# The laying out of substitution rows in the heads' delta rule: one fp32 matmul, or two fp32r matmuls over a high and a low part

## What is computed

```python
low = jnp.einsum('nbhik,nbhjk->nbhij', kb, kc) * decay_strict
t_inv = lax.linalg.triangular_solve(low + eye, eye, left_side=True, lower=True, unit_diagonal=True)
u = jnp.einsum('nbhij,nbhjv->nbhiv', t_inv, vb)
```

## Time and profile before

| | |
|---|---|
| median of 3 runs | 1622.85 us (1619.63 to 1623.05) |
| the profiled execution | 1618.03 us |
| its span | 1616.2 us |
| TensorE busy | 1586.6 us, 98% of the span |
| VectorE busy | 986.1 us, 61% |
| GpSimd busy | 154.3 us, 10% |

### The profile page before, as it was taken

How to read it: one execution, slowest core, us unless ns; L and a number is a source line. 1 busy time by engine, 2 the same in 40 slices (tenths; PEclk the granted TensorE clock), 3 DMA queues, 4 the chain that set the end, 5 groups by cost and what they waited for, 6 DMA issues and landing times.

```text
span 1616.2 us, 29865 instructions
## 1 busy us (share of the span) xinstructions
PE 1586.6 (98%) x11971; PEld 1435.0 (89%) x11971; DVE 986.1 (61%) x1685; ACT 636.7 (39%) x1094; POOL 154.3 (10%) x170
## 2 busy tenths in 40 slices
PE   7999999999999999999999999999999999799997
PEld 6887899999999999999999999999999998577765
DVE  5676447766867668577445654444498865533455
ACT  5666445442543425434332232222244434422422
POOL 0121000121112111121100001111100000000000
PEclk9999999999999999999999999999999999999999
DMA  7798754332433323333369975888813348978764
GB/s 274 251 296 261 239 136 121 80 95 56 118 94 79 94 65 107 95 77 106 81 166 235 246 186 140 218 218 210 218 48 107 93 127 299 363 257 289 243 247 163
DMA packets 344206, 274.64 MB, mean 170 GB/s; under 512 B 50953, under 2 KB 291490, under 8 KB 343090
## 3 DMA queue, kind: packets, MB, share of 16 engines
q1 hardware_dynamic: 321648, 256.48, 54.2%
q10 hardware_dynamic: 22466, 16.88, 3.8%
HBM read 229.50 MB, written 44.17 MB: 169 GB/s over the span
## 4 chain that ended last, share of the span: by engine, by line
PE 92%; DVE 3%; DMA 2%; issue 1%; ACT 1%; SPq 1%; ACTq 0%; DVEq 0%
PE pj L283 47%; PE pj L508 11%; PE dk L3009 6%; PE pj L2349 5%; PE dk L2349 3%; PE pj L2968 3%; PE pj L2976 1%; PE dk L2631 1%; DMA w_raw_co<-in_w_co_dram 1%; PE pj L2670 1%; PE dk L1955 1%; PE dk L1332 1%; PE dk L368 1%; PE pj L2653 1%; DVE q_both L2255 1%
## 5 line engine op out<-in xcount | busy, mean ns | idle before, releaser
L283 PE MATMUL pj<-a_hi,w_high 128*128 128x272 f32 x1664 | 364.6, 300 | 0.3 <-DVE w_low L267 0.2
L283 PE MATMUL pj<-a_hi,w_low 128*128 128x272 f32 x1664 | 343.6, 288 | 0.0
L283 PE MATMUL pj<-a_lo,w_high 128*128 128x272 f32 x1664 | 343.2, 288 | 0.0
L283 PEld LDWEIGHTS pj<-a_hi,w_high 128*128 128x128 f32 x1664 | 259.5, 189 | 12.7 <-issue 7.8
L283 PEld LDWEIGHTS pj<-a_lo,w_high 128*128 128x128 f32 x1664 | 261.4, 188 | 0.0
L283 PEld LDWEIGHTS pj<-a_hi,w_low 128*128 128x128 f32 x1664 | 260.1, 189 | 0.0
L267 DVE TENSOR_TENSOR w_low<-w_raw,w_high 128x2048 fp32r<-128x2048 f32 x68 | 155.4, 2286 | 77.0 <-ACT w_high L257 76.9
L257 ACT ACTIVATE w_high<-w_raw 128x2048 fp32r<-128x2048 f32 x68 | 130.4, 1917 | 73.6 <-PE pj L283 42.4
L283 PE MATMUL pj<-mix_hi,w_high 128*128 128x272 f32 x512 | 105.9, 288 | 0.1
L283 PE MATMUL pj<-mix_lo,w_high 128*128 128x272 f32 x512 | 105.4, 288 | 0.0
L283 PE MATMUL pj<-mix_hi,w_low 128*128 128x272 f32 x512 | 105.1, 287 | 0.0
(11 more groups left out here) (460 smaller groups left out, 2890.9 us busy)
## 6 DMA issues: line engine op xcount, KB each, us to landing
w_raw<-in_w_in_dram SPq DMA_DIRECT2D x48, 1024.0 KB, 5.8
w_raw_co<-in_w_co_dram SPq DMA_DIRECT2D x28, 1024.0 KB, 7.4
w_raw_wide<-in_w_ck_dram SPq DMA_DIRECT2D x16, 1024.0 KB, 6.9
w_raw_wide<-in_w_cv_dram SPq DMA_DIRECT2D x16, 1024.0 KB, 7.5
w_raw<-in_w_out_dram SPq DMA_DIRECT2D x16, 1024.0 KB, 6.9
keys_s<-keysT_scratch SPq DMA_DIRECT2D x7, 2048.0 KB, 10.2
values_s<-in_cache_mem_v_dram SPq DMA_DIRECT2D x28, 512.0 KB, 8.2
q_part<-in_w_cq_dram SPq DMA_DIRECT2D x48, 256.0 KB, 3.6
```

The lines of the kernel that those rows point to most:

```text
L283: mm = pe.matmul(pj[:, 2 * (q % 2) + b, 0:n], wt[:, k, :], x(k, o, n), start=(k == 0 and m == 0), stop=(k == KT - 1 and m == 2))
```

## The change

The strips are laid out by two fp32r matmuls per bank in place of one fp32 matmul. VectorE rounds `comp` to `comp_high`, subtracts it from `comp` for `comp_low`, and spreads `comp_high` over the strips `own_high`. GpSimd spreads `comp_low` over the strips `own_low`. TensorE waits for both and adds the two products in the same bank. The last strip gets four rows in place of three (60 elements in place of 45).

```diff
-strip_rows = lambda r: min(4, BLK - 1 - 4 * r)
+strip_rows = lambda r: 4
...
+        def own_strip(eng, dst, src, r):
+
+            m, w = strip_rows(r), strip_width(r)
+            return eng.tensor_tensor(dst, src[:, :, BLK - w:BLK].unsqueeze(2).to_broadcast([P, CH + 1, m, w]),
+                                     cst[:, C_E16 + 4 * r:C_E16 + 4 * r + m].unsqueeze(1).unsqueeze(3).to_broadcast(
+                                         [P, CH + 1, m, w]), ALU.mult)
...
                 dve.wait_ge(comp_ready, n + 1)
+                dve.tensor_copy(comp_high[:], comp[:]).then_inc(comp_cast, 1)
+                dve.wait_ge(comp_cast, n + 1)
+                dve.tensor_tensor(comp_low[:], comp[:], comp_high[:].bitcast(F32), ALU.subtract).then_inc(comp_split, 1)
                 for r in range(4):
-                    m, w = strip_rows(r), strip_width(r)
-                    a = dve.tensor_tensor(strip(own_row, r), comp[:, :, BLK - w:BLK].unsqueeze(2).to_broadcast([P, CH + 1, m, w]),
...
+                    a = own_strip(dve, strip(own_high, r), comp_high[:].bitcast(F32), r)
                 a.then_inc(own_ready, 1)
...
             if q == 1:
+                pool.wait_ge(comp_split, n + 1)
+                for r in range(4):
+                    a = own_strip(pool, strip_low(r), comp_low, r)
+                a.then_inc(own_rest, 1)
                 old()
...
-                blk = cst[:, C_BLK:C_BLK + P]
+                pe.wait_ge(own_rest, n + 1)
                 for b in range(2):
                     e = strip_size(b) + strip_size(b + 2)
-                    mm = pe.matmul(dk[:, b, 0:e], blk, own_row[:, b, 0:e], start=True, stop=True)
+                    pe.matmul(dk[:, b, 0:e], blk_r[:], own_high[:, b, 0:e], start=True, stop=False)
+                    mm = pe.matmul(dk[:, b, 0:e], blk_r[:], own_low[b][:, 0:e], start=False, stop=True)
```

More of the change, by code:

```diff
@@ L730, in build @@
         betab = take("betab", [TOK])
+        dd_at = take.pos[0]
         dd = take("dd", [2, TOK])
@@ L744, in build @@
         ksv = put("ksv", [2, P], F32, take.pos[0] - 2 * TOK + 4 * CH * T32)
-        own_row = put("own_row", [2, OWN_BANK], F32, take.pos[0] - 2 * TOK)
+        own_high = put("own_high", [2, OWN_BANK], F32R, take.pos[0] - 2 * TOK)
         assert 2 * OWN_BANK <= 2 * TOK
@@ L751, in build @@
         ones_r = take("ones_r", [P], F32R)
+        blk_r = take("blk_r", [P], F32R)
+        comp_high, comp_low = take("comp_high", [CH + 1, BLK], F32R), take("comp_low", [CH + 1, BLK])
+        own_low = [put("own_low0", [OWN_BANK], F32R, dd_at + TOK), put("own_low1", [strip_size(1) + strip_size(3)], F32R, vbk_at)]
+        assert OWN_BANK <= TOK and strip_size(1) + strip_size(3) <= SEQ
         SQ = put("sq", [2, TOK], F32, fold_at)
@@ L800, in build @@
         ks_taken, kqs_ready = sem("ks_taken"), sem("kqs_ready")
+        comp_cast, comp_split, own_rest = sem("comp_cast"), sem("comp_split"), sem("own_rest")
         kds_copied, vns_copied = Reused(squared, 7), Reused(rooted, 7)
@@ L1126, in strip, with strip_low @@
             return x[:, r % 2, o:o + n].rearrange("p (c j i) -> p c j i", c=CH + 1, j=strip_rows(r))
+        def strip_low(r):
+            o, n = (0 if r < 2 else strip_size(r - 2)), strip_size(r)
+            return own_low[r % 2][:, o:o + n].rearrange("p (c j i) -> p c j i", c=CH + 1, j=strip_rows(r))
+        def own_strip(eng, dst, src, r):
[3 more added lines that the diff above has]
+                                         [P, CH + 1, m, w]), ALU.mult)
         def substitute(eng, n):
@@ L1145, in dve_delta @@
                     dve.tensor_copy(ones_r[:], ones)
+                    dve.tensor_copy(blk_r[:], cst[:, C_BLK:C_BLK + P])
                 dve.wait_ge(qk_silu, n + 1)
@@ L1181, in dve_delta @@
                 dve.wait_ge(comp_ready, n + 1)
+                dve.tensor_copy(comp_high[:], comp[:]).then_inc(comp_cast, 1)
+                dve.wait_ge(comp_cast, n + 1)
+                dve.tensor_tensor(comp_low[:], comp[:], comp_high[:].bitcast(F32), ALU.subtract).then_inc(comp_split, 1)
                 for r in range(4):
-                    m, w = strip_rows(r), strip_width(r)
-                    a = dve.tensor_tensor(strip(own_row, r), comp[:, :, BLK - w:BLK].unsqueeze(2).to_broadcast([P, CH + 1, m, w]),
-                                          cst[:, C_E16 + 4 * r:C_E16 + 4 * r + m].unsqueeze(1).unsqueeze(3).to_broadcast(
-                                              [P, CH + 1, m, w]), ALU.mult)
+                    a = own_strip(dve, strip(own_high, r), comp_high[:].bitcast(F32), r)
                 a.then_inc(own_ready, 1)
```

## The result

The changed kernel took 1628.32 us (median of 8 runs) against 1622.74 us: ratio 1.0036, 95% interval 1.0019 to 1.0052. It is slower, as forecast, but by 5.6 us where 12.9 were expected.

A forecast was written before the change was run, and what follows sets the result against it. TensorE, busy 98%, was taken to bound the kernel, with VectorE's run to `t_next` only 0.06 us shorter in six heads; 10.2 us for heads 1 to 6, 1.44 and 1.23 made 12.9, so 1635.8 us, range 1625.5 to 1644.

The forecast's parts named there:

- TensorE saves 0.52 us per head, if it could be kept: TensorE's strip matmuls: four fp32r passes take 0.67 us in place of 1.19, 4.2 us in all.
- The cast and the subtraction delay the first strip by 0.40 us: VectorE ahead of its strips: two new instructions make the first strip start 0.40 us later, at 359.52.
- Whole instructions, in turns: VectorE's and GpSimd's strips, both reading two SBUF tensors, alternate by whole instructions; adds 1.24 us to VectorE's delay.
- Substitution starts 1.66 later: VectorE's first substitution step: the strips' whole delay of 1.66 us is carried over to it.
- Slack 0.06 us at `t_next`: TensorE's wait at `level32_p`, heads 1 to 6: VectorE's delay less 0.06 us makes TensorE late.
- 0.1 us per head for a broken stream: TensorE at a wait that binds: breaking its stream costs up to 0.2 us, taken as 0.1 per head.
- The sum: All heads: 1.70 us in each of heads 1 to 6, 1.44 in head 0, 1.23 in the last; together 12.9 us.
- No taking of turns: Rival, strips: VectorE's run through first, GpSimd's follow; VectorE late by 0.42 us, 3.0 us in all, 1625.8; chance 0.14.
- Dear short runs on GpSimd: Rival, GpSimd's strips: short runs cost 3 ns per column; 19.8 us in all, 1642.6; chance 0.17.
- Faster, because the wait does not decide: Rival, `level32_p`: TensorE passes the wait in time and keeps 0.52 us per head, 4.2 us, 1618.7; chance 0.06.
- The case that was forecast: Strips taking turns, GpSimd at 1.7 to 2.2 ns per column: 1635 to 1639 us; chance 0.63.
- the range for 8 in 10: Whole kernel time: from the case without turns, 1625.5, to a little above dear short runs, 1644 us.

The follow-up runs named there:

- high_only: Changed kernel with the low part left out (no cast, subtraction or low strips, one fp32r pass per bank); ratio 0.9986 against the kernel before.
- pool_later: Changed kernel with GpSimd's four strips made to wait for VectorE's last strip, nothing else; ratio 1.0105 against the kernel before.
- the second timing: The same changed kernel timed again without any edit against the kernel before; ratio 1.0056 (1.0035 to 1.0077).

## Why the prediction was right in kind and wrong in size

The direction, the mechanism and its place were right; the size was not, 12.9 us against 5.6 in the first comparison, 9.1 in the heads. The step that failed is the one from VectorE's delay to TensorE's: 1.66 us at the strips, carried over whole to the first step of the substitution and on to TensorE, at 1.70 us per head. The runs showed 1.49 us at `kds`, 1.27 at the first step and 1.18 at TensorE.

*TensorE saves 0.52 us per head, if it could be kept.* Right: 1.19 became 0.65, and high_only shows that it cannot be kept behind VectorE's list as it is.

*The cast and the subtraction delay the first strip by 0.40 us.* Right: it starts 0.40 us after the cast does (360.00 and 360.40), in the place where it started before.

*Whole instructions, in turns.* Right, by the forms' durations and by pool_later. The term was mis-sized: VectorE's strips got 1.08 us longer in place of 1.24 and 0.02. Read in the same way as above over all of head 1, GpSimd's first three strips cost 0.55 + 0.41 + 0.27 = 1.23 us (1.30 worked out) and VectorE's last three 0.24 + 0.17 + 0.08 = 0.49 (0.59): once it has its turn, VectorE needs hardly more than its columns at 1.04 ns, and I had added 0.05 us to each.

*"Substitution starts 1.66 later."* This is where it failed most. With the strips' true share `kds` is 1.49 us late, and the first step started only 1.27 us later. In the earlier trace rows the first step starts at 364.25, after the split's end at 364.10, because it waited there for TensorE's slow fp32 matmuls, which end at 364.11. The kernel before, VectorE and TensorE, head 1:

```profile
361.83 2.27 DVE L267 TENSOR_TENSOR w_low<-w_raw,w_high 128x2048 fp32r<-128x2048 f32 x1
```

```profile
362.76 1.35 PE L1348 MATMUL dk<-own_row,cst 128*128 128x440 f32 x4
```

In the changed kernel the last of the four matmuls is over by 365.28, and the first step starts at 366.40, just as the split runs out. high_only bears this out: there the first step starts 4.93 us after the first strip, against 5.13 before, with no added work on VectorE but the 15 elements of the last strip. I had called TensorE's step "in time" after the change and not asked whether it had been so before. So the shorter matmuls did pay something: 0.2 us per head, on VectorE's path.

*Slack 0.06 us at `t_next`, the delay paid nearly whole.* Right: in heads 5 and 6 `t_next` is 1.25 us later, and TensorE starts `level32_p` 31.22 to 31.23 us after the norms in place of 30.04, 1.18 us later. Over heads 1 to 6 it is 1.12 to 1.25.

*0.1 us per head for a broken stream.* Wrong: 1.25 less 0.06 is 1.19, so the break costs nothing there.

*The sum.* Per inner head 1.70 us became 1.18: 0.18 from the turns, 0.22 from the first step, 0.1 from the break, 0.02 from rounding. The seven heads and the last one together give 9.1 us. What remains down to 5.6 stands in no trace: the interval of the first timing ends at 8.4 us, the second timing gave 8.9. So 3.8 of the 7.3 us by which the forecast missed are accounted for, and the rest stays open.

*The rivals.* No taking of turns: excluded by the groups of L1142. Dear short runs on GpSimd: excluded; in pool_later 300 and 220 columns differ by 133 ns, 1.7 ns per column with runs of 15 and 11 elements. Faster, because the wait does not decide: excluded by high_only. The case that was forecast, 1635 to 1639 us, did not hold; the range for 8 in 10, 1625.5 to 1644, took in the measured 1628.3 only by its lower edge, which came from the excluded case without turns, and that is luck. The sum came out too high because the break and VectorE's fixed time, both unmeasured, were taken too large, and what the quicker matmuls give back to VectorE was put at nothing without a look at the rows before.

What stays open is the rule by which the turns are given. Among the strips it is first come, first served by the recorded starts (GpSimd's second at 361.37, VectorE's third at 361.58, in all eight heads and each of the three places); in pool_later the later record won in seven heads of eight. Whether GpSimd's order of strips (small ones first) would have changed anything wasn't tried.

## What to carry to other kernels

Ask of a saving on the busiest engine how far behind the next path is. Look for it at waits that cause no idle time yet: the distance between a producer's end and the wait it serves was 0.06 us here, and it decided more than the 0.5 us that was saved. An instruction moved to GpSimd is not taken off VectorE if both read two tensors from SBUF at that time; put it beside VectorE's work from PSUM, or on ScalarE. And when a step gets quicker, list who had been waiting for it before, since that is where its gain comes back.

## What the runs showed of the hardware

A GpSimd instruction of 140 columns took 2.82 us on average beside a VectorE instruction of 2.27 us, in seven heads of eight one that started 0.31 us later by the record. ScalarE's small activations with a scale column cost 0.23 us from start to start on average (16 in 3.68 us), from 0.25 us at 75 columns down to 0.20 us at 15.

In pool_later the 2.4 us for which TensorE stood idle in each head had a second price. In heads 2, 6 and 7 of eight the granted clock fell after it, to 1.2 GHz, and came back within 5 us; head 2, in windows of 2 us (busy time by engine, then the granted clock):

```profile
434.00:436.00 2.00, 0.36 (x2) 0.38 (x3) 0.97 (x1) 0.00 (x0) 1.49 (x2) 1.00 0.00 0
436.00:438.00 2.00, 2.00 (x14) 1.99 (x13) 1.16 (x5) 0.00 (x0) 0.00 (x0) 0.74 0.00 0
438.00:440.00 2.00, 2.00 (x11) 2.00 (x11) 1.73 (x8) 0.00 (x0) 0.00 (x0) 0.50 0.00 0
440.00:442.00 2.00, 2.00 (x17) 2.00 (x16) 1.71 (x9) 0.00 (x0) 0.00 (x0) 0.91 0.00 0
```

TensorE is idle in most of the first window and in the next three runs at 0.74, 0.50 and 0.91 of its full clock. The head took 70.1 us where its neighbours took 68.7 to 68.8. Idle times of 0.8 us per head, in the changed kernel, left the clock at 1.00 throughout the stretch. What sets heads 2, 6 and 7 apart from the five whose clock stayed is not shown.
